# Order of the opening loads: the first value chunk and the first query chunk in turns

## The reference, cut to what matters

```python
proj = jnp.einsum('bsd,dc->bsc', x, w_in[l]).astype(f32)
q_a, k_a, v_a, q_b, k_b, v_b = jnp.split(proj, splits, axis=-1)
q_a = apply_rope(q_a.reshape(B, S, N_HEADS_DIFF, 2, DIFF_QK_DIM), cos_a, sin_a)
...
o_a = diff_attention(q_a, k_a, v_a, lam, subln_g[l], lambda_init)
...
o_b = dilated_attention(q_b, k_b, v_b)
mix = jnp.concatenate([o_a.reshape(B, S, DIFF_WIDTH), o_b.reshape(B, S, DIL_WIDTH)], axis=-1)
attn_out = jnp.einsum('bsc,cd->bsd', mix, w_out[l])
x = layer_norm(DEEPNORM_ALPHA * x + attn_out, ln1_g[l], ln1_b[l])
hdn = jnp.square(jax.nn.relu(jnp.einsum('bsd,df->bsf', x, w_ff1[l])))
ff_out = jnp.einsum('bsf,fd->bsd', hdn, w_ff2[l])
x = layer_norm(DEEPNORM_ALPHA * x + ff_out, ln2_g[l], ln2_b[l])
```

## Time and profile before

| | us |
|---|---|
| median of 3 runs | 1097.82 (1097.68 to 1098.16) |
| the profiled execution | 1098.61 |
| its span, first to last instruction | 1096.8 |
| TensorE busy in it | 1082.0 (99%) |
| VectorE, ScalarE, GpSimd busy | 810.7, 568.5, 25.0 |

### The profile page before, as it was taken

How to read it: one execution, slowest core, us unless ns; L and a number is a source line. 1 busy time by engine, 2 the same in 40 slices (tenths; PEclk the granted TensorE clock), 3 DMA queues, 4 the chain that set the end, 5 groups by cost and what they waited for, 6 DMA issues and landing times.

```text
span 1096.8 us, 13843 instructions
## 1 busy us (share of the span) xinstructions
PE 1082.0 (99%) x5579; PEld 918.2 (84%) x5579; DVE 810.7 (74%) x891; ACT 568.5 (52%) x715; POOL 25.0 (2%) x45
## 2 busy tenths in 40 slices
PE   9999999999999999999999999999999999999995
PEld 7888888888888878888888888888888888888884
DVE  6577757756656685667699898666766669989988
ACT  6577756655554524455455454344454446554550
POOL 1000101000000000000000000000000000000001
PEclk9999999999999999999999999999999999999998
DMA  9856655675555834665656557466666656655762
GB/s 292 255 183 216 188 176 157 177 244 173 170 172 166 283 107 154 192 187 178 218 186 229 194 192 240 159 190 185 186 179 206 190 170 215 230 192 192 247 251 77
DMA packets 109823, 213.83 MB, mean 195 GB/s; under 512 B 6768, under 2 KB 41840, under 8 KB 109248
## 3 DMA queue, kind: packets, MB, share of 16 engines
q1 hardware_dynamic: 109136, 209.74, 59.5%
q0 software_dynamic: 624, 3.21, 1.0%
HBM read 210.83 MB, written 2.10 MB: 194 GB/s over the span
## 4 chain that ended last, share of the span: by engine, by line
PE 96%; DVE 2%; DMA 1%; SPq 1%; issue 1%; POOL 0%; ACT 0%; POOLq 0%; DVEq 0%
PE low_ps L584 11%; PE low_ps L713 11%; PE high_ps L713 9%; PE high_ps L733 8%; PE high_ps L732 8%; PE high_ps L731 8%; PE low_ps L589 6%; PE low_ps L477 5%; PE low_ps L718 5%; PE low_ps L481 5%; PE low_ps L479 5%; PE high_ps L718 5%; PE low_ps L733 2%; PE low_ps L732 2%; PE low_ps L731 2%; PE high_ps L524 1%
## 5 line engine op out<-in xcount | busy, mean ns | idle before, releaser
L1154 DVE TENSOR_TENSOR w_lo<-w_raw,w_hi 128x1024 fp32r<-128x1024 f32 x174 | 212.2, 1223 | 132.7 <-ACT w_hi L858 131.7
L858 ACT ACTIVATE w_hi<-w_raw 128x1024 fp32r<-128x1024 f32 x174 | 184.2, 1059 | 186.5 <-PE low_ps L481 64.6
L584 PE MATMUL low_ps<-xT,w_hi 128*128 128x512 f32 x512 | 179.4, 397 | 0.0
L713 PE MATMUL low_ps<-x1T,w_hi 128*128 128x512 f32 x512 | 176.7, 393 | 0.0
L713 PE MATMUL high_ps<-x1T,w_hi 128*128 128x512 f32 x448 | 155.0, 394 | 0.0
L589 PE MATMUL low_ps<-xT,w_lo 128*128 128x256 f32 x512 | 139.8, 283 | 0.0
L718 PE MATMUL low_ps<-x1T,w_lo 128*128 128x256 f32 x512 | 136.9, 278 | 0.0
L1472 DVE TENSOR_TENSOR w_lo<-w_raw,w_hi 128x1024 fp32r<-128x1024 f32 x72 | 87.1, 1222 | 64.5 <-ACT w_hi L1049 64.5
L1049 ACT ACTIVATE w_hi<-w_raw 128x1024 fp32r<-128x1024 f32 x72 | 76.1, 1060 | 88.7 <-PE low_ps L713 43.4
L718 PE MATMUL high_ps<-x1T,w_lo 128*128 128x256 f32 x448 | 119.8, 278 | 0.0
L731 PE MATMUL high_ps<-w_hi,hid 128*128 128x512 f32 x288 | 112.0, 389 | 0.0
(11 more groups left out here) (186 smaller groups left out, 1833.0 us busy)
## 6 DMA issues: line engine op xcount, KB each, us to landing
w_raw<-in_w_ff SPq DMA_DIRECT2D x208, 512.0 KB, 4.3
w_raw<-in_w_in SPq DMA_DIRECT2D x92, 512.0 KB, 3.9
more_raw<-in_w_ff SPq DMA_DIRECT2D x44, 512.0 KB, 5.2
w_raw<-in_w_out SPq DMA_DIRECT2D x32, 512.0 KB, 3.7
x_raw<-in_x_turned SPq DMA_DIRECT2D x8, 256.0 KB, 7.2
w_raw<-in_w_in SPq DMA_DIRECT2D x8, 256.0 KB, 6.1
y<-in_x SPq DMA_DIRECT2D x8, 256.0 KB, 4.4
side_raw<-in_w_ff SPq DMA_DIRECT2D x4, 512.0 KB, 6.7
```

The lines of the kernel that those rows point to most:

```text
L584: return pe.matmul(banks[:, b, :], w_hi[:, slot, cols], xT[:, t, :, :].rearrange("p h t -> p (h t)"), start=(t == 0), stop=(t == KT - 1))
L713: return pe.matmul(banks[:, b, :], w_hi[:, slot, cols], x1T[:, t, :, :].rearrange("p h t -> p (h t)"), start=(t == 0), stop=(t == KT - 1))
L858: act.activation(w_hi[:, slot, :], w_raw[:, slot, :], ACT.Copy).then_inc(w_rounded, units)
L1154: dve.tensor_tensor(w_lo[:, slot, :], w_raw[:, slot, :], w_hi[:, slot, :].bitcast(F32), ALU.subtract).then_inc(w_split, units)
```

## The change

The first 12 entries of `IN_UNITS` get another order: (value 0), (value 1), (query 0), (value 2), (value 3), (query 1), and so on, so that the value chunk ends with unit 10 and the query chunk with unit 11. Only units 0 and 1 are handled in halves (`HALVED = 2`, in place of SLOTS = 4); unit 2, the first query unit, and unit 3 are handled whole. The pairs of x are loaded, rounded and split in the places where their value units now stand. The copy of the values moves from `attention_after` at n = 7 to n = 10, in front of `step(10)` and behind the lambda block. Unit 12 and all after it keep their places.

```diff
--- before.py
+++ after.py
@@ -56,6 +56,9 @@
     IN_PLAN += [(2, group, 0)] + pairs if group == 0 else pairs + [(2, group, 0)]
 IN_UNITS = [(c, k) for c, (which, group, half) in enumerate(IN_PLAN)
             for k in range(UPH if which == 2 else KT // KQ)]
+OPENING = UPH + KT // KQ
+HALVED = 2
+IN_UNITS[:OPENING] = [of for k in range(KT // KQ) for of in ((0, 2 * k), (0, 2 * k + 1), (1, k))]
 CHUNK_END = [max(u for u, (c, k) in enumerate(IN_UNITS) if c == i) for i in range(len(IN_PLAN))]
 
 ROPE_CHUNK = [i for i, (which, group, half) in enumerate(IN_PLAN) if which < 2]
@@ -260,7 +263,7 @@
     side_loaded = [sem(f"side_loaded{s}") for s in range(SLOTS)]
     side_rounded, side_split = sem("side_rounded"), sem("side_split")
 
-    half_loaded = [sem(f"half_loaded{k}") for k in range(SLOTS)]
+    half_loaded = [sem(f"half_loaded{k}") for k in range(HALVED)]
     half_rounded, half_split = sem("half_rounded"), sem("half_split")
     w_rounded, w_split, w_used = sem("w_rounded"), sem("w_split"), sem("w_used")
     ident_loaded, tables_loaded = sem("ident_loaded"), sem("tables_loaded")
@@ -359,22 +362,25 @@
         if which == 2:
             load_chunk_unit(sp, w_in_d, u, k, chunk, u % SLOTS)
             return
-        sp.wait_ge(w_split, u - (SLOTS - 1))
+        if u >= SLOTS:
+            sp.wait_ge(w_split, u - (SLOTS - 1))
         sp.dma_start(w_raw[:, u % SLOTS, :].rearrange("p (k n) -> p k n", k=KQ),
                      w_qk_d[:, k, :, 2 * chunk + half, :]).then_inc(w_loaded[u % SLOTS], 16)
 
     def sync_program(sp):
 
-        for k in range(UPH):
-            pair = slice(KU * k, KU * (k + 1))
-            sp.dma_start(x_raw[:, pair, :], x_turned[:, pair, :]).then_inc(x_loaded[k], 16)
-            if k < SLOTS:
-                for kk, loaded in enumerate((half_loaded[k], w_loaded[k])):
-                    sp.dma_start(w_raw[:, k, kk * NC:(kk + 1) * NC],
+        for u in range(OPENING):
+            c, k = IN_UNITS[u]
+            if c == 0:
+                pair = slice(KU * k, KU * (k + 1))
+                sp.dma_start(x_raw[:, pair, :], x_turned[:, pair, :]).then_inc(x_loaded[k], 16)
+            if u < HALVED:
+                for kk, loaded in enumerate((half_loaded[u], w_loaded[u])):
+                    sp.dma_start(w_raw[:, u, kk * NC:(kk + 1) * NC],
                                  w_in_d[:, k, kk, in_chunk(2), :]).then_inc(loaded, 16)
             else:
-                load_in_unit(sp, k)
-        for u in range(UPH, U_OUT):
+                load_in_unit(sp, u)
+        for u in range(OPENING, U_OUT):
             load_in_unit(sp, u)
             if u in X_AT:
 
@@ -950,7 +956,7 @@
                 copy_low(ROPE_AFTER.index(n))
             if n - 1 in ROPE_AFTER:
                 rotate(ROPE_AFTER.index(n - 1))
-            if n in VALUES_AFTER:
+            if n in VALUES_AFTER[1:]:
                 copy_v(VALUES_AFTER.index(n))
             if n in PROBS_AT:
                 copy_probsT(PROBS_AT.index(n))
@@ -965,17 +971,25 @@
             if n - 1 in VALUES_AT and VALUES_AT.index(n - 1) < N_DIFF:
                 scale_output(VALUES_AT.index(n - 1))
 
-        for k in range(SLOTS):
-            round_x(k)
+        def round_opening(u):
+
+            c, k = IN_UNITS[u]
+            if u < OPENING and c == 0:
+                round_x(k)
+
+        for k in range(HALVED):
+            round_opening(k)
             for kk, (loaded, rounded) in enumerate(((half_loaded[k], half_rounded),
                                                     (w_loaded[k], w_rounded))):
                 cols = slice(kk * NC, (kk + 1) * NC)
                 act.wait_ge(loaded, 16)
                 act.activation(w_hi[:, k, cols], w_raw[:, k, cols], ACT.Copy).then_inc(rounded, 1)
-        for k in range(SLOTS):
-            round_x(SLOTS + k)
-            step(k)
-        for n in range(SLOTS, U_OUT + UPH * (CHUNKS - 1)):
+        for u in range(HALVED, SLOTS):
+            round_opening(u)
+            round_unit(u, u, 1)
+        for n in range(U_OUT + UPH * (CHUNKS - 1)):
+            if n + SLOTS < OPENING:
+                round_opening(n + SLOTS)
             if n == UPH + 2:
                 act.wait_ge(lam_loaded, 16 * 5)
                 act.activation(subln_scaled, subln, ACT.Copy,
@@ -983,6 +997,8 @@
                 act.wait_ge(lam_summed, 2)
                 act.activation(lam_exp, lam_sum, ACT.Exp).then_inc(lam_exped, 1)
             attention_before(n)
+            if n == VALUES_AFTER[0]:
+                copy_v(0)
             step(n)
             attention_after(n)
 
@@ -1268,17 +1284,23 @@
         dve.memset(zeros[:, :], 0.0).then_inc(zeroed, 1)
         dve.memset(minus_half, -0.5).then_inc(powers_ready, 1)
         dve.memset(eps_sum, HEAD_DIM * EPS).then_inc(powers_ready, 1)
-        for k in range(SLOTS):
-            split_x(k)
+        def split_opening(u):
+
+            c, k = IN_UNITS[u]
+            if c == 0:
+                split_x(k)
+
+        for k in range(HALVED):
+            split_opening(k)
             for kk, (rounded, split) in enumerate(((half_rounded, half_split),
                                                    (w_rounded, w_split))):
                 cols = slice(kk * NC, (kk + 1) * NC)
                 dve.wait_ge(rounded, k + 1)
                 dve.tensor_tensor(w_lo[:, k, cols], w_raw[:, k, cols], w_hi[:, k, cols].bitcast(F32),
                                   ALU.subtract).then_inc(split, 1)
-        for k in range(SLOTS):
-            split_x(SLOTS + k)
-            ahead(0, k)
+        for u in range(HALVED, SLOTS):
+            split_opening(u)
+            split_unit(u, u)
 
         def lam_sums():
             dve.wait_ge(lam_loaded, 16 * 5)
@@ -1296,9 +1318,9 @@
                                      op1=ALU.subtract).then_inc(lam_ready, 1)
             dve.wait_ge(lam_ready, 1)
 
-        for k in range(SLOTS, UPH):
-            ahead(0, k)
-        attention_after(UPH - 1)
+        for u in range(SLOTS, OPENING):
+            split_opening(u)
+            ahead(0, u - SLOTS)
         for n in range(UPH, U_OUT + OUT_END[0] - 1):
             attention_before(n)
             ahead(0, n)
```

## The result

The changed kernel takes 1100.62 us (median of 11 executions, 1099.05 to 1101.75), the kernel before 1098.00 (11 executions, 1097.29 to 1098.73): ratio 1.0023, 95% interval 1.0016 to 1.0031. It is slower by 2.6 us. The forecast was 1099.3, with a range of 1098.0 to 1101.0. The profiled execution took 1100.03, its span is 1098.2.

A forecast was written before the change was run, and what follows sets the result against it. TensorE, 96% of the chain, was taken as the bound, so the effect was unit 12's shift: the larger of +0.79 (TensorE) and +1.46 (copy). Median 1097.82 + 1.46 = 1099.3 us, range 1098.0 to 1101.0.

The forecast's parts named there:

- The step that decides: ScalarE's copy of the values, behind the lambda block and unit 13's load, starts at 41.08 and holds unit 12 until 42.30.
- +1.46: Forecast delay in us of unit 12's start on TensorE, 42.30 in place of 40.84, set by the late copy.
- Later constants, later copy: Rival, 14%: unit 13's landing moves with GpSimd's later start, or unit 2 lands past 12.8; +2.3 us, 1100.1.
- The landing of unit 2: The whole first query unit's load lands at 11.40, bounds 10.63 to 12.08, so its first product starts at 13.88.
- Loads land in the order of their bytes: Rule for the opening loads: unit 2, ending at 2.0 MB like the old half unit, lands at 11.40 too.
- Its own sign of being wrong: The prediction called itself wrong if unit 2's w_hi rounding started far from 11.4; two other signs were named.
- the hole up to 13.9: TensorE idle from 11.29 until unit 2's first product; with the slow first product 2.67 us in place of 1.88.
- Faster: Rival, 5%: unit 2 lands at 9.6, TensorE gains 1.0 us, and the copy doesn't wait; 1096.8.
- The sum: Median before 1097.82 plus 1.46 gives 1099.3; from the profiled span, 1098.3 and a time of 1100.1.
- TensorE's own way: When TensorE by itself would finish unit 11: 41.63, +0.79 us; as the rival that this counts, 12%, 1098.6.
- The clock falls: Rival, 8%: idle TensorE near 11.3 drops the clock to 1.2 GHz, costing 2.6 beyond 0.79; +3.4 us, 1101.2.
- Small parts: Fewer, larger roundings, splits and DMA issues; units 14 and 15's rounding and chunk 1's rope 1.0 later, all taken as hidden.

The follow-up runs named there:

- set 3: The changed kernel run again, unedited; median 1100.99 us, ratio 1.0029 to the kernel before.
- set 8: The changed kernel run again, unedited, for a fourth set; median 1101.57 us, ratio 1.0026 to the kernel before.
- experiment 1: The changed kernel with the copy of the values one step earlier, in front of the rounding of unit 13; 1098.06 us, ratio 1.0000 to the kernel before.
- experiment 2: The kernel before, in its old order of units, with only the copy of the values moved behind the lambda block; 1100.26 us, ratio 1.0020.
- experiment 9: The changed kernel with the copy of the values before the lambda block, still behind unit 13's rounding; 1098.48 us, ratio 1.0004 to the kernel before.
- set 5: The changed kernel run again, unedited, for a third set; median 1100.37 us, ratio 1.0027 to the kernel before.
- experiment 10: The changed kernel with GpSimd waiting for 8 used units in place of 5 before issuing the constants; 1101.27 us, ratio 1.0029 to the kernel before.

## Why the prediction was right, and where its size was off

**The step that decides was right.** The median moved by 2.6 us, inside the range of 1098.0 to 1101.0, but by 1.8 times the +1.46 that was forecast. The range reached that far for the rival *Later constants, later copy* (+2.3), and its cause did not come: unit 13 was rounded at 37.80. So it is in part luck that the number lies in the range; the sets 3 and 8 have medians of 1100.99 and 1101.57 (1100.92 without the execution of 6213 us), at its very edge. What is right is the mechanism. The prediction put the cost at the copy of the values behind the lambda block, behind unit 13's load, and not in the opening. Its times against the profile: rounding of unit 13 37.96 and 37.80, exponential 40.97 and 40.81, copy 41.08 and 40.92, unit 12 42.30 and 41.98 + 0.10 for the slower first product. The argument that unit 13 lands at the same time whatever the order of the bytes ahead of it held to 0.3 us (37.80, 38.22, 38.25 and 37.87 in four profiles). Experiments 1, 2 and 9 show the cause: the copy's place alone makes the difference, in either order.

**The landing of unit 2 was wrong,** without weight in the sum. "Loads land in the order of their bytes", with 11.40 for the 2.0 MB, failed: unit 2 is rounded at 9.62, 9.39 and 9.65 in three profiles of the changed kernel and at 11.01 in the fourth. Over the nine profiles with this opening, those of the experiments with it, it is rounded at 9.39 to 11.31; in the old order the half unit that ends at 2.0 MB is rounded at 11.38 in the profile before and at 10.41 in experiment 2. The prediction took the landing of one execution for that of the kernel, and a late one. Its own sign of being wrong, a rounding of unit 2 far from 11.4, came true, and the hole up to 13.9 that it announced is not there in the first profile. 9.6 is the landing of the rival *Faster* (TensorE 1.0 earlier). That rival also wanted a copy that doesn't wait, and with one (experiment 1) the gain still did not come. What makes the lag stays open.

**The sum was mis-sized in its base.** The copy sets a time of day for unit 12, not a delay on top of the old one. The prediction added +1.46, the shift of unit 12 against one profiled execution that stood 0.8 above the median, to the median. TensorE's own way varies: over the nine profiles with this opening it could have begun unit 12 at 39.8 to 41.5. With the late copy it begins it at 42.0 to 42.4 in all four profiles. So an execution that was quick before loses more than +1.46. That the 0.8 of the profile before lay ahead of unit 12 is argued, not shown. The sum against the span gave 1100.1, and the 18 executions without the fall have the median 1099.98, +1.9 on before.

**The clock was the term that the sum put at nothing.** The rival *The clock falls* had 8%, outside the range, and looked at the wrong hole: the one at 11.3 that hardly came to be. It priced a fall at 2.6, from the kernel's start; measured is 3.4 us at half the clock, of which 1.7 are lost. The hole that the forecast itself made at 40 us, taken as 0.7 because unit 2 was thought late, is 1.98 to 2.42 when unit 2 is early (1.05 in set 3, where it is late), and 14 of 32 executions are 1.8 longer, by the two profiled ones because of a fall behind it. 18 at +1.9 and 14 at +3.7 are +2.7 on the mean. An early landing thus gives nothing: each microsecond that TensorE gains in the opening makes the hole before the copy longer. Whether a longer hole makes the fall likelier no run tests by itself; in experiment 2, with a hole of 1.48, one of nine executions is at 0.994. The Trainium skill ("TensorE: Matmul & The Clock Gate", section "Why this matters for your kernels") warns of idle gaps between bursts of matmuls, but of longer ones than these. In sets 5 and 8 the clock fell at gaps of 2.42 and 2.05 us all the same, and the measurement decides.

**Small parts.** The later rounding of units 14 and 15 and the later rope cost 0.1 at most: the span behind unit 12 is 1056.2 against 1056.0, with 0.1 for the slower first product.

## What to carry to other kernels

When a step is moved in an engine's hand-written order, read what it now stands behind on that engine, and for what that waits; here a copy whose data was ready waited 2 us for a scalar's sums and through them for a load. A wait that is set by a load gives unit 12 a fixed time, so put its price against the time at which the work would otherwise start in a typical execution, not in the one profiled. And a new hole on TensorE can have two prices, its length and that of a fall of the clock in some executions: look at the mean granted clock of every execution, not only at the profiled one.

## What the runs showed of the hardware

The granted clock fell from 1.00 to 0.50 for 3.4 us (2.4 to 1.2 GHz) at holes of 1.81, 2.05 and 2.42 us, and did not at one of 1.98 us in the first profile of the changed kernel, of 1.83 us in experiment 10's or of 1.72 us in set 3's; so a hole of 2 us may or may not cost 1.7 us more. In set 5 the fall began at 43.8, when TensorE had been at work again for 1.4 us, and in set 8 at 41.9, inside the hole. The rounding of unit 2, which follows its landing, came at 9.39 to 11.31 in nine profiles with the same opening. And with 8 products (16 records) added to TensorE at 40 us a load at 1065 us landed 1.1 to 1.6 us later in both profiles (6.38 and 6.87 against 5.25), with an instruction packet moved while it was under way; that the packet is the cause is not shown.
